# Scores and maxima one block ahead, v projected inside attention, first norm from token rows, two rotation buffers

## The reference

```
xn = rms_norm(h, attn_norm_g[l]);  q, k, v, u = split(xn @ w_in[l])      # widths 512, 128, 128, 512
q = apply_rope(rms_norm(q, q_norm_g[l]), cos, sin) * q_scale             # 8 heads of 64
k = apply_rope(rms_norm(k, k_norm_g[l]), cos, sin)                       # 2 key heads
attn = sliding_sink_attention(q, k, v, sinks[l])  # chunks of 64 see themselves, the chunk before, the 16 meta tokens
pool = multiscale_pool(u, w_pool[l], pool_scale[l])  # 4 groups of 128: mean of the last 2, 4, 8, 16 minus u; a 128x128 map
h = h + concat(attn, pool) @ w_out[l]
xn = rms_norm(h, ffn_norm_g[l])
g = causal_dwconv(xn @ w_gate[l], conv_w[l], conv_b[l])
h = h + (gelu(g) * (xn @ w_up[l])) @ w_down[l]                           # width 2816
```

## Time and profile before

| what | us |
|---|---|
| runs | 1099.22, 1100.20, 1102.31; median 1100.2 |
| the profiled execution, its own time | 1100.07 |
| its span, first to last instruction | 1098.3 |
| busy in the span: PE, DVE, ACT, POOL | 1064.2, 522.4, 471.3, 123.3 |

### The profile page before, as it was taken

How to read it: one execution, slowest core, us unless ns; L and a number is a source line. 1 busy time by engine, 2 the same in 40 slices (tenths; PEclk the granted TensorE clock), 3 DMA queues, 4 the chain that set the end, 5 groups by cost and what they waited for, 6 DMA issues and landing times.

```text
span 1098.3 us, 18457 instructions
## 1 busy us (share of the span) xinstructions
PE 1064.2 (97%) x7668; PEld 1001.0 (91%) x7668; DVE 522.4 (48%) x690; ACT 471.3 (43%) x662; POOL 123.3 (11%) x121
## 2 busy tenths in 40 slices
PE   6998899999999999999999989999999999999997
PEld 6897799999999999999999978999988999888886
DVE  5667645545445545232336576455455544532221
ACT  5775435444444444122237664364344543421110
POOL 1262000111000111000003510000001100000000
PEclk9989999999999999999999899999999999999999
DMA  6311222322322322323321112223223232233212
GB/s 201 103 49 40 77 77 77 103 89 77 114 76 76 105 86 70 103 78 105 104 78 49 39 40 97 96 77 108 84 76 114 77 111 80 76 106 106 72 61 77
DMA packets 93518, 94.30 MB, mean 86 GB/s; under 512 B 3392, under 2 KB 91800, under 8 KB 93480
## 3 DMA queue, kind: packets, MB, share of 16 engines
q1 hardware_dynamic: 92768, 93.01, 26.4%
q0 software_dynamic: 400, 0.58, 0.2%
q10 hardware_dynamic: 312, 0.18, 0.1%
HBM read 91.65 MB, written 2.10 MB: 85 GB/s over the span
## 4 chain that ended last, share of the span: by engine, by line
PE 82%; ACT 8%; DVE 7%; issue 1%; DMA 1%; SPq 0%; POOL 0%; DVEq 0%; ACTq 0%; POOLq 0%
PE slot L443 80%; ACT probs L919 3%; ACT w_hi L337 1%; DVE nmax L1170 1%; DMA x_in<-in_x 1%; ACT rot_s L844 1%; DVE ms_work L1121 1%; DVE probs L1189 1%; DVE w_lo L348 1%; DVE mix_lo L1205 0%; ACT x_hi L778 0%; DVE den L1181 0%; DVE sumsq L1046 0%; DVE sink_arg L1175 0%; ACT pool_hi L852 0%
## 5 line engine op out<-in xcount | busy, mean ns | idle before, releaser
L443 PE MATMUL slot<-x_hi,w_hi 128*128 128x264 f32 (+1 forms) x1552 | 364.1, 302 | 5.4 <-DVE x_lo L1033 2.7
L443 PE MATMUL slot<-x_lo,w_hi 128*128 128x264 f32 (+1 forms) x1552 | 361.0, 300 | 0.0
L443 PE MATMUL slot<-x_hi,w_lo 128*128 128x264 f32 (+1 forms) x1552 | 360.2, 299 | 0.0
L348 DVE TENSOR_TENSOR w_lo<-raw,w_hi 128x2048 fp32r<-128x2048 f32 (+2 forms) x87 | 194.6, 2237 | 247.6 <-ACT w_hi L337 247.6
L337 ACT ACTIVATE w_hi<-raw 128x2048 fp32r<-128x2048 f32 (+3 forms) x89 | 160.8, 1806 | 260.8 <-PE slot L443 259.5
L443 PEld LDWEIGHTS slot<-x_hi,w_hi 128*128 128x128 f32 x1552 | 254.4, 190 | 17.4 <-DVE u_sb L1152 3.9
L443 PEld LDWEIGHTS slot<-x_lo,w_hi 128*128 128x128 f32 x1552 | 253.0, 190 | 7.3
L443 PEld LDWEIGHTS slot<-x_hi,w_lo 128*128 128x128 f32 x1552 | 252.6, 191 | 7.4
L443 PE MATMUL slot<-m_hi,w_lo 128*128 128x264 f32 (+1 forms) x528 | 140.7, 321 | 0.0
L443 PE MATMUL slot<-m_hi,w_hi 128*128 128x264 f32 (+1 forms) x528 | 140.4, 320 | 0.0
L443 PE MATMUL slot<-m_lo,w_hi 128*128 128x264 f32 (+1 forms) x528 | 140.3, 320 | 0.0
(11 more groups left out here) (142 smaller groups left out, 931.3 us busy)
## 6 DMA issues: line engine op xcount, KB each, us to landing
raw<-in_w_gate SPq DMA_DIRECT2D x44, 512.0 KB, 4.6
raw<-in_w_up SPq DMA_DIRECT2D x44, 512.0 KB, 4.4
raw<-in_w_down SPq DMA_DIRECT2D x32, 512.0 KB, 4.3
raw<-in_w_in SPq DMA_DIRECT2D x19, 512.0 KB, 4.9
raw<-in_w_out SPq DMA_DIRECT2D x16, 512.0 KB, 4.5
raw<-in_w_down SPq DMA_DIRECT2D x16, 384.0 KB, 3.6
x_in<-in_x SPq DMA_DIRECT2D x4, 512.0 KB, 7.7
out<-y_out SPq DMA_DIRECT2D x8, 256.0 KB, 3.0
```

What stands on the lines that cost most here:

```text
L348: ins = nc.vector.tensor_tensor(w_lo[s][:, a:b], raw[s][:, a:b], w_hi[s][:, a:b].bitcast(f32), ALU.subtract)
L443: ins = nc.tensor.matmul(out_part, w[ws][:, r, cols], a[:, k, tokens], start=first and n == 0 and w is w_hi and a is a_hi, stop=end and w ...
```

## The change

The weight units of the input projection are paired anew, k and q3, q1 and q2, q0 and u3, v and u0, u1 and u2; the third is loaded as two DMAs of 128 columns. PE's order is k, norm, q0, k's mean, q1, q2, `q_means(0)`, q3, u3, `q_means(1)`, `scores(0)`, v, and then the steps, whose step 1 begins with the transposes of v. No side rows precede the steps. The first layer's norm is computed from the row tiles: ACT squares `x_in` and sums along the row, takes a root, DVE inverts, PE spreads the numbers over the partitions with five small matmuls, ACT copies them to rinv; the squares and the DVE additions of that norm go. SP instead of POOL loads the large half of the constants. Sine, `rot_c` and `rot_s` have two buffers each, and a rotation waits for the one two before it. In step s PE issues `scores(s+1)` and DVE does `row_maxima(s+1)` behind `divide(s-1)`. The first pooling map goes through the side slot in two halves. The pooling groups come in the order 3, 0, 2, 1.

```diff
-U_KV, U_Q, U_U23, U_U01, U_POOL, U_OUT = 0, 1, 3, 4, 5, 6
+U_KQ3, U_Q12, U_Q0U3, U_VU0, U_U12, U_POOL, U_OUT = 0, 1, 2, 3, 4, 5, 6
...
-            order += [(f"scores{b}", 1 - b % 2)] + {5: [("pool3", 1)], 8: [("pool2", 0), ("pool1", 0)]}.get(b, [])
+            order += [(f"scores{b}", b % 2)] + {8: [("pool0", 1), ("pool2", 1)]}.get(b, [])
...
-            sine = v_T[:]
-            rot_c = sb(sc, "rot_c", [P, L])
-            rot_s = sb(sc, "rot_s", [P, L])
+            sine = [v_T[:], run_b[:, PAD:]]
+            rot_c = [sb(sc, f"rot_c{n}", [P, L])[:] for n in range(2)]
+            rot_s = [sb(sc, "rot_s", [P, L])[:], run_a[:, PAD:]]
...
-        GROUPS = (3, 2, 1, 0)
+        GROUPS = (3, 0, 2, 1)
-        SIDE_ENDS = [5, 8, 14, 20, 26, 32, 38, 44, 48, 48, 48, 48, 48]
+        SIDE_ENDS = [0, 0, 7, 14, 21, 28, 34, 41, 48, 48, 48, 48, 48]
-        POOLED_AT, POOL_HI_AT, POOL_LO_AT, MAP_AT = (1, 4, 6, 9), (2, 5, 7, 9), (3, 6, 9, 9), (5, 8, 9, 10)
+        POOLED_AT, POOL_HI_AT, POOL_LO_AT, MAP_AT = (2, 4, 7, 9), (3, 5, 8, 9), (4, 6, 9, 9), (5, 8, 9, 10)
...   # SP
+            sp.dma_start(cst[:, C_CNT:], const[:, C_CNT:]).then_inc(const_loaded, 16)
+                sp.dma_start(raw[s][:, :, 0:P], win[:, :, 0:P]).then_inc(raw_loaded[s], 16)
+                sp.dma_start(raw[s][:, :, P:UC], win[:, :, IN_WIDTH - P:IN_WIDTH]).then_inc(raw_loaded[s], 16)
...   # PE
+                else:
+                    s = open_slot("attn_norm", 0)
+                    pe.wait_ge(row_inv, 1)
+                    for t, (bank, c0, n) in enumerate(ROW_TILES):
+                        ins = nc.tensor.matmul(slot[s][:, bank, c0:c0 + n], row_ms[0:n, t:t + 1].broadcast_to([n, P]),
+                                               ident[0:n, 0:n], start=True, stop=True)
+                project("q0", U_KQ3)
...
+                project("q1", U_Q12)
+                project("q2", U_Q12)
                 q_means(0)
+                project("q3", U_Q0U3)
+                project("u3", U_Q0U3)
+                q_means(1)
...
+                scores(0)
+                project("v", U_VU0)
                 for step in range(NB + 2):
-                    if step < NB:
-                        scores(step)
+                    if step == 1:
+                        v_transposed()
+                    if step == MAP_AT[1]:
+                        pool_map(1)
...
                     project_side(first, min(cut, end))
+                    if step + 1 < NB:
+                        scores(step + 1)
                     if step >= 2:
                         heads(step - 2)
+                    if step == MAP_AT[0]:
+                        first_map(0)
...
                     if 1 <= step <= NB:
                         probs_T(step - 1)
+                    if step == MAP_AT[0]:
+                        first_map(1)
                     project_side(cut, end)
...
-                rows = [(k, k) for k in (7, 6, 5, 0, 1, 2, 3, 4)]
+                rows = [(k, k) for k in (7, 4, 6, 0, 1, 2, 3, 5)]
...   # POOL
-                    if n > 0:
-                        pool.wait_ge(*rotated_before(l, n))
+                    if n >= 2:
+                        pool.wait_ge(*rotated(l, n - 2))
...   # ACT, prologue
+                act.wait_ge(x_loaded[t], 16)
+                nc.scalar.activation(y_out[:, t], x_in[:, t], ACT.Square, accum_out=row_ms[:, t:t + 1])\
+                  .then_inc(row_summed, 1)
...
+            act.wait_ge(filled[s], ps.before("attn_norm", 0) + 1)
+            nc.scalar.activation(rinv[:, 0:N_META + 3 * P], slot[s][:, 0, 0:N_META + 3 * P], ACT.Copy)
+            nc.scalar.activation(rinv[:, N_META + 3 * P:], slot[s][:, 1, 0:P], ACT.Copy).then_inc(evac[s], 1)
             split_hi(act, 0, 1)
-            for k in range(KT):
-                square(0, 0, k)
...   # ACT, projections (only the order of these calls changes)
                 q_squares(0)
+                split_hi(act, l, 2)
                 shift(0)
                 shift(1)
                 q_squares(1)
+                shift(2)
                 split_hi(act, l, 3)
+                q_rms(0)
+                q_squares(2)
+                shift(3)
...   # k_win copies
                 q_squares(3)
                 shift(4)
                 q_rms(1)
+                split_hi(act, l, 4)
...   # ACT, steps
+                    if step == 1:
+                        v_windows()
                     if step < NB:
                         exps(step)
+                    if step == MAP_AT[0]:
+                        for half in range(2):
+                            first_map_hi(half)
...   # DVE
-            for k in range(KT):
-                add_square(0, 0, k)
...
-                scaled("v", v_T[:])
...
                 q_tile(1)
+                sine_part(2)
+                split_lo(dve, l, 2)
...   # the four additions into k_dup
-                sine_part(2)
+                q_tile(2)
+                sine_part(3)
                 split_lo(dve, l, 3)
+                q_tile(3)
+                sine_part(4)
...
+                row_maxima(0)
+                split_lo(dve, l, 4)
                 for step in range(NB + 3):
+                    if step == 0:
+                        dve.wait_ge(*shifted(l, 4))
+                        scaled("v", v_T[:])
...
                     if 1 <= step <= NB:
                         divide(step - 1)
-                    if step < NB:
-                        row_maxima(step)
+                    if step + 1 < NB:
+                        row_maxima(step + 1)
...
+                    if step == MAP_AT[0]:
+                        for half in range(2):
+                            first_map_lo(half)
```

More of the change, by code:

```diff
@@ new lines, in _, with v_transposed @@
+                project("u3", U_Q0U3)
+                q_means(1)
+                def v_transposed():
+                    s = open_slot("v_T", l)
+                    pe.wait_ge(evac[ps.slot("v")], ps.before("v", l) + 1)
+                    flat = slot[s][:].rearrange("p a t -> p (a t)")
+                    for w in range(NWIN):
+                        t0 = N_META + w * CHUNK
+                        nc.tensor.transpose(flat[:, w * P:(w + 1) * P], v_T[:, t0:t0 + P], ident)
+                    nc.tensor.transpose(flat[0:N_META, NWIN * P:(NWIN + 1) * P], v_T[:, 0:N_META], ident)\
+                      .then_inc(filled[s], 1)
@@ L537, in project_side, with first_map @@
                             ins.then_inc(filled[4], 1)
+                def first_map(half):
+                    g = GROUPS[0]
+                    name = f"pool{g}{'ab'[half]}"
+                    open_slot(name, l)
+                    if half == 0:
+                        pe.wait_ge(lo_split[U_POOL % 2], slot_turn(l, U_POOL) + 2)
+                        pe.wait_ge(plo_ready, l * 4 + 1)
+                    dense(None, U_POOL % 2, (g % 2) * P, [(g // 2, 0)], pool_hi, pool_lo, part=half)\
+                      .then_inc(filled[4], 1)
                 def pool_map(n):
@@ L849, in pooled_hi, with first_map_hi @@
                     if n >= 2:
-                        name = f"pool{GROUPS[n - 2]}"
+                        name = f"pool{GROUPS[n - 2]}" + ("b" if n == 2 else "")
                         act.wait_ge(filled[ps.slot(name)], ps.before(name, l) + 1)
                     nc.scalar.activation(pool_hi[:, n % 2], pooled[:, n % 2], ACT.Copy).then_inc(phi_ready, 1)
+                def first_map_hi(half):
+                    g, h0 = GROUPS[0], half * HALF
+                    act.wait_ge(filled[4], ps.before(f"pool{g}{'ab'[half]}", l) + 1)
+                    nc.scalar.activation(mix_hi[:, 4 + g, h0:h0 + HALF], side, ACT.Copy,
+                                         scale=par[:, R_PS + g:R_PS + g + 1]).then_inc(mixhi_ready, 1)
                 def pool_map_hi(n):
@@ L907, in _, with v_windows @@
                 q_rms(1)
+                split_hi(act, l, 4)
+                def v_windows():
+                    s = ps.slot("v_T")
+                    act.wait_ge(filled[s], ps.before("v_T", l) + 1)
+                    flat = slot[s][:].rearrange("p a t -> p (a t)")
+                    act.wait_ge(vmeta_zero, l + 1)
+                    for t in range(4):
+                        j2, kv = divmod(t, 2)
+                        nc.scalar.activation(v_meta[t * META_ROWS:t * META_ROWS + N_META, kv,
+                                                    j2 * HEAD_DIM:(j2 + 1) * HEAD_DIM],
+                                             flat[0:N_META, NWIN * P + kv * HEAD_DIM:NWIN * P + (kv + 1) * HEAD_DIM],
+                                             ACT.Copy)
+                    nc.scalar.activation(v_win[:, 0:4].rearrange("p w d -> p (w d)"), flat[:, 0:4 * P], ACT.Copy)
+                    nc.scalar.activation(v_win[:, 4:NWIN].rearrange("p w d -> p (w d)"), flat[:, 4 * P:NWIN * P],
+                                         ACT.Copy).then_inc(evac[s], 1)
                 def exps(b):
@@ L951, in _ @@
```

(8 more changed lines are left out.)

216 lines of the change are left out of this document (97 added, 119 removed).

## The result

| | before | after |
|---|---|---|
| median of the runs | 1100.38 (11 runs, 1099.22 to 1104.86) | 1103.97 (11 runs, 1102.73 to 1105.95) |
| profiled execution, its own time | 1100.07 | 1104.76 |
| its span | 1098.3 | 1103.0 |

The change makes the kernel 0.27% slower: the ratio is 1.0027, 95% interval 1.0014 to 1.0039. That is just under the 0.3% named in the prediction, but the interval does not reach down to 1, so a small loss is measured. The forecast was 1095.3 with a range up to 1101.

A forecast was written before the change was run, and what follows sets the result against it. PE was taken as the bound, busy 97% of the span. Front, middle and tail summed to gains of 2.6 us in layer 0 and 2.2 in layer 1, together 4.8 off 1100.07: 1095.3, range 1087 to 1101.

The forecast's parts named there:

- the tail: PE's step 8 to the output projection: 13.55 us a layer, a loss of 0.2 in layer 0, 1.6 in layer 1.
- my walk: Step-by-step tracing of the engines' queues through each stage; in the tail it put exps(8) ending 5.65 us into step 8.
- The middle: scores(0) to PE's step 8: 47.95 us a layer, a gain of 1.6 in layer 0, 1.2 in layer 1.
- That loop is open: Attention steps: maxima a block ahead end the exps, division, maxima loop, so PE bounds at about 5 us per step.
- The front: k to scores(0): 45.55 us in layer 0, a gain of 1.2; 41.9 in layer 1, a gain of 2.6.
- the slow clock charged at 0.8: Front: 0.8 us added for half clock, since one of two first q_means was followed by a slow stretch.
- The rotation comes late: Rival, chance 0.11: before scores(0), POOL and DVE collisions delay the rotation, costing 5.2 us a layer: 1105.7.
- the slack of 1.5: Front, layer 1: POOL's additions for q3 end at 600.4, PE reaches scores(0) at 601.9, leaving 1.5 us.
- The time only changes place: Rival, chance 0.17: 6.7 us slow stretches stay behind the second q_means, side waits gain at most 0.3 a layer: 1099.0.
- The steps run at PE's pace: Rival, chance 0.17: in the steps, waits shrink from 3.75 to 1 us and tails stay as before: 1086.5.

The follow-up runs named there:

- experiment 1: Changed kernel with the third pooled tile rounded on ACT before the last exps, not behind them: 1100.04 us, ratio 0.9998 to the kernel before.
- experiment 2: Changed kernel with the third pooled tile made on DVE behind the division of block 7, so POOL's last sums start later: 1100.28 us, ratio 0.9994.
- experiment 4: Kernel before with only scores and maxima moved one block ahead of values and division: 1104.79 us, ratio 1.0057.
- experiment 10: Kernel before with scores and maxima one block ahead and the u half's exit in front of the maxima on DVE: 1094.44 us, ratio 0.9946.
- the mended kernel: Changed kernel with third pooled tile later, its rounding earlier, first map whole through slot 0, and u half ahead of the maxima: 1086.61 us, ratio 0.9875.
- experiment 9: The mended kernel with scores and maxima not one block ahead, the u half still in front of the maxima: 1100.15 us, ratio 0.9999.
- experiment 3: Changed kernel with the first pooling map made whole through score slot 0 at the start of step 5, not in two halves: 1098.56 us, ratio 0.9977.
- experiment 6: Changed kernel with its two rotation buffers used one at a time, each rotation waiting for the one before it: 1114.91 us, ratio 1.0132.
- experiment 8: The run of the mended kernel, all four edits together on the changed kernel: 1086.61 us, ratio 0.9875.
- the square of the kernel before: Kernel before with scores and maxima ahead or not, u half or maxima first on DVE; ratios: neither 1, ahead 1.0057, half first 1.0108, both 0.9946.
- experiment 11: Kernel before with only the u half's exit put in front of the maxima on DVE, nothing ahead: 1113.80 us, ratio 1.0108.

## Why the prediction was wrong

- **The step that failed: the tail.** "On my walk exps(8) end 5.65 after step 8 begins, the rounding 6.2, ..." The exps ended 7.1 after. The walk had the right queue (the rounding behind exps(8), which experiment 1 shows by taking it out) but two durations too small: the division of block 7 was priced without POOL's last sums beside it, 0.15 and 0.23 for what took 0.78 and 0.96, and exps(8) wait for transposes that wait for that division. I had weighed exactly this contention, but for the rotations alone. Then the clock: 0.7 charged, 10 and 7 us at half clock measured. Instead of 13.55 the tails took 15.88 and 15.85, 4.6 us together. The late exps(8) are 1.5 of the 2.3 us in each layer, and experiment 2, which takes only this contention away, shortens each by 1.5.
- **The middle: waits as priced, work mis-sized.** I charged 3.75 us of waits a layer, v's exit and the side slot. Layer 1 shows 0.72 for v, then 0.61, 0.56, 0.55 and 1.10 = 3.54, layer 0 0.36, 0.60, 0.57, 0.55 and 1.10 = 3.18. The three of step 5 are at the named places; of the four charged before them (0.75, 0.15, 0.1, 0.2) one came, with 0.6. Layer 1 took 1.0 more than forecast all the same, and layer 0 2.1 more, of which its half-clock stretch inside step 5 (24 side matmuls in 4.65 us instead of 3.11) is 1.5. Without the waits and with 1.7 for the stretch behind scores(0), as charged, some 43.7 us are left in either layer where the sum had 41.2 + 1.3 = 42.5. So PE's own work with its short blocks was put 1.2 too low a layer; no run shows which part of it. What I did not see is that the waits could be taken away for nothing: I wrote that the half "is queued behind row_maxima(s+1), which waits for PE's scores(s+1)", and then only priced it. Experiments 4 and 10 show that in the kernel before this order turns a part worth 5.9 us into one that costs 6.3.
- **"That loop is open": right as a mechanism.** Before's ACT waits 2.20 and 2.99 us for the maxima in the blocks shown above; in layer 1 of after it waits 0.36 us before block 0 and not at all from block 1 on. That this pays is shown in the kernel before (experiment 10). In the mended kernel experiment 9 changes ahead and leaves an order that suits only ahead, so its 13.6 us mix the two.
- **The front: right, with some luck in the terms.** scores(0) began 0.4 us later than forecast in layer 0 (63.38 for 63.0) and the front of layer 1 took 41.59 for 41.9, with 0.58 and 0.55 of wait on POOL against 0.5. k began 0.27 later, not 0.6. In layer 1 the slow clock charged at 0.8 did not come, so the rest took 0.4 longer than the walk. In layer 0 the front from k's own start is 0.7 longer than forecast, and the slow start of k accounts for it (last finding below): experiments 1 to 3, which touch nothing there, have 44.6 to 44.7. The second buffers carry the front: experiment 6.
- **The rivals.** "The rotation comes late" did not happen, although its contention did: k's four additions took 5.00 us instead of 2.85 (row below), and the slack of 1.5 and other work took it up. Its number, 1105.7, is the nearest to the measured one, by chance. "The time only changes place" (1099.0) has its name right and its sign wrong: the stretches behind the second q_means shrank to 4 and 3.5 us, and the slow time moved to the tails. "The steps run at PE's pace" had 1086.5, where experiment 8 has 1086.6, but with other orders of the queues, so the match says nothing for it.
- **Between the stages and behind them** I had nothing, and 0.43 and 1.12 us came. The half-clock stretch of the last tail runs 1.6 us on into the output projection (670.37 to 672), which is 0.8; the rest no run explains.

How far does the clock go? After adds 3 us of half-clock time to before's 24.5 by the windows, and its k ran its first 5.4 us at half pace while the column read 1.00 (finding below), which makes 33. If PE works through a stretch it costs half its length, so some 4 of the 4.7 us are clock. This is an estimate from the stretches, and an upper one, for PE also waits in the tails. It overlaps with the causes above, since experiments 1 and 2 change waits and stretches at once. The same sum can be made for the square of the kernel before: 24.5 us of slow stretches (neither), about 35 (ahead), 41.5 (half first) and 15.5 (both; 10.5 by the column and 5.0 of a slow start of k that it misses). By halves that is +5, +8.5 and -4.5 us, beside spans that differ by +4.7, +14.2 and -6.7. Much of what an order costs or gains is thus paid in clock. That waits and slow stretches mostly go together the runs show (14 us in experiment 8, 41.5 and 52.5 in experiments 11 and 6), though not always: experiment 3 took waits out and its profiled execution had some 35 us. That the waits bring the stretches about is argued, since no run changed the one without the other.

## What to carry to other kernels

When one stage is pulled ahead, reorder every queue that serves it: an engine that empties several results should take them in the order in which the producer issues them, and each pair of changes belongs in one experiment, since here the one alone costs 6 us, the other alone 12, and both together gain 6. In a tail walked, ask of each DVE duration what POOL does at that moment, and of each short job whether it stands behind a long one that waits. A wait priced in a forecast is also a place where the order can be mended.

## What the hardware showed

- DVE and POOL hinder each other at every size seen here, from 4 columns to 2048. POOL loses too: its sum of 16 columns at 657.62 took 0.68 us beside the division, and 0.22 in experiment 2 (656.74). Four additions of 528 columns into k_dup took 5.00 us in after beside two rotations, and 2.85 in before with POOL idle:

```profile
589.09 5.00 DVE L1197 TENSOR_TENSOR k_dup<-rot_c,run_a 64x528 f32<-64x528 f32 x4
```

- The stretches at a granted clock of 0.5 come in lengths of about 3.5, 7 and 10 us, and 14 in experiments 3 and 6. The orders of the same work run here had between 10.5 and 52.5 us of them in the two attention stages, by the clock column.
- The clock column can miss a slow stretch. At the start of k in after a pair of matmuls took 0.44 us from start to start, as at half clock, up to 23.1 us, and 0.24 from 23.5 on, while the windows from 17 to 24 read 1.00. Experiment 10 shows the same from 16.94 to 21.9. The distance of starts is the surer sign:

```profile
21.81 0.64 PE L460 MATMUL slot<-x_hi,w_hi 128*128 128x264 f32 x2
22.25 0.64 PE L460 MATMUL slot<-x_lo,w_hi 128*128 128x264 f32 x2
...
23.96 0.41 PE L460 MATMUL slot<-x_hi,w_hi 128*128 128x264 f32 x2
24.20 0.41 PE L460 MATMUL slot<-x_lo,w_hi 128*128 128x264 f32 x2
```
